# Dense logits in one visit at step 13, four places for the row maxima, lambda's sums two steps earlier

## The reference

```python
qa, ka, va, qi, ki, wi, ga, qb, kb, vb, gb = _split_in(h @ w_in[i])
oa = _dsa_attention(qa, ka, va, qi, ki, wi, top_k)     # sparse: top 64 keys by an indexer
lam_init = 0.8 - 0.6 * math.exp(-0.3 * i)
lam = (jnp.exp(jnp.sum(lambda_q1[i] * lambda_k1[i]))
       - jnp.exp(jnp.sum(lambda_q2[i] * lambda_k2[i])) + lam_init)
ob = _diff_attention(qb, kb, vb, lam, lam_init, subln_g[i])
y = jnp.concatenate([oa * jax.nn.silu(ga), ob * jax.nn.silu(gb)], axis=-1) @ w_out[i]
x = x + _rmsnorm(y, post_norm_g[i])
# then: x = x + rmsnorm((p[i] @ w_ple_proj[i]) * sigmoid(x @ w_ple_gate[i]))

# the dense (differential) group, per block of 128 queries, chunk-causal over 256 keys:
probs = jax.nn.softmax(jnp.where(allowed, logits, NEG_INF), axis=-1)
attn = (probs[:, 0] - lam * probs[:, 1]).astype(v.dtype)
out = _rmsnorm(attn @ v, sub_g) * (1.0 - lam_init)
```

## Time and profile before

| | us |
|---|---|
| median of 3 runs | 357.84 (357.63 to 358.26) |
| the profiled execution | 358.45 |
| its span | 356.7 |
| TensorE's matmuls busy | 348.7 (98% of the span) |
| VectorE busy | 263.6 (74%) |
| ScalarE busy | 229.0 (64%) |
| GpSimd busy | 68.0 (19%) |

### The profile page before, as it was taken

How to read it: one execution, slowest core, us unless ns; L and a number is a source line. 1 busy time by engine, 2 the same in 40 slices (tenths; PEclk the granted TensorE clock), 3 DMA queues, 4 the chain that set the end, 5 groups by cost and what they waited for, 6 DMA issues and landing times.

```text
span 356.7 us, 5705 instructions
## 1 busy us (share of the span) xinstructions
PE 348.7 (98%) x1927; PEld 292.0 (82%) x1927; DVE 263.6 (74%) x562; ACT 229.0 (64%) x459; POOL 68.0 (19%) x121
## 2 busy tenths in 40 slices
PE   8999999999999999999999999999999999999992
PEld 7897888888888788888888888788888888888882
DVE  2886979988875676786797577988895658678543
ACT  4797567686577945555667564787666796365221
POOL 1066351142200000003105624004230000000000
PEclk9999999999999999999999999999999999999997
DMA  7996479862744464657575927546356336550011
GB/s 265 380 360 191 125 224 175 285 173 67 196 160 148 146 195 159 203 167 154 182 226 155 349 82 208 161 122 180 115 146 208 115 130 228 176 169 10 2 48 69
DMA packets 31820, 61.12 MB, mean 171 GB/s; under 512 B 2376, under 2 KB 4432, under 8 KB 31792
## 3 DMA queue, kind: packets, MB, share of 16 engines
q1 hardware_dynamic: 30656, 57.48, 50.3%
q0 software_dynamic: 1120, 3.28, 4.8%
q10 hardware_dynamic: 16, 0.00, 0.0%
HBM read 59.71 MB, written 1.05 MB: 170 GB/s over the span
## 4 chain that ended last, share of the span: by engine, by line
PE 94%; issue 2%; DMA 1%; DVE 1%; ACT 0%; POOLq 0%; DVEq 0%; POOL 0%; SPq 0%
PE proj L1249 26%; PE proj L1251 25%; PE proj L1250 25%; PE sc L1330 3%; PE tr L1398 2%; PE tr L1348 2%; PE sc L1182 2%; PE pv L1415 1%; DMA raw<-in_w_ple_proj_dram 1%; PE proj L1166 1%; PE proj L1193 1%; PE pv L1420 1%; PE proj L1182 1%; PE proj L1262 1%; PE proj L1155 1%
## 5 line engine op out<-in xcount | busy, mean ns | idle before, releaser
L1249 PE MATMUL proj<-w_hi,act_hi 128*128 128x512 f32 (+1 forms) x392 | 157.1, 401 | 0.0
L1251 PE MATMUL proj<-w_hi,act_lo 128*128 128x512 f32 (+1 forms) x392 | 152.2, 388 | 0.0
L1250 PE MATMUL proj<-w_lo,act_hi 128*128 128x512 f32 (+1 forms) x392 | 151.6, 387 | 0.0
L849 DVE TENSOR_TENSOR w_lo<-raw,w_hi 128x1024 fp32r<-128x1024 f32 (+1 forms) x102 | 121.3, 1208 | 10.5 <-ACT w_hi L610 9.9
L610 ACT ACTIVATE w_hi<-raw 128x1024 fp32r<-128x1024 f32 (+2 forms) x103 | 102.4, 1023 | 3.3 <-PE proj L1251 1.8
L1251 PEld LDWEIGHTS proj<-w_hi,act_lo 128*128 128x128 f32 x392 | 73.6, 188 | 15.5
L1249 PEld LDWEIGHTS proj<-w_hi,act_hi 128*128 128x128 f32 x392 | 73.7, 188 | 14.3 <-issue 0.7
L1250 PEld LDWEIGHTS proj<-w_lo,act_hi 128*128 128x128 f32 x392 | 73.8, 188 | 12.8
L551 POOL TENSOR_TENSOR rstd<-var,minus_half 128x1 f32<-128x1 f32 x12 | 7.6, 639 | 190.8 <-DVE var L837 161.4
L746 ACT ACTIVATE probs<-probs,neg_max 128x128 f32<-128x128 f32 (+1 forms) x64 | 28.2, 444 | 4.8 <-DVE neg_max L1000 4.8
L541 POOL TENSOR_TENSOR v_all<-work,rot_tab 128x128 f32<-128x128 f32 x16 | 10.6, 662 | 76.8 <-ACT work L610 76.6
(11 more groups left out here) (229 smaller groups left out, 450.1 us busy)
## 6 DMA issues: line engine op xcount, KB each, us to landing
raw<-in_w_in_dram SPq DMA_DIRECT2D x59, 512.0 KB, 4.1
raw<-in_w_out_dram SPq DMA_DIRECT2D x16, 512.0 KB, 3.3
raw<-in_w_ple_gate_dram SPq DMA_DIRECT2D x16, 512.0 KB, 3.8
raw<-in_w_in_dram SPq DMA_DIRECT2D x7, 324.0 KB, 5.0
raw<-in_w_ple_proj_dram SPq DMA_DIRECT2D x4, 512.0 KB, 4.1
resid<-in_x_dram SPq DMA_DIRECT2D x2, 512.0 KB, 7.1
probs<-in_w_in_dram SPq DMA_DIRECT2D x2, 512.0 KB, 9.3
g_ple<-in_ple_norm_g_dram POOLq DMA_DIRECT2D x2, 512.0 KB, 8.0
```

What stands on the lines that cost most here:

```text
L849: nc.vector.tensor_tensor(w_lo[:, g % SLOTS, 0:nk * cols], landing(g, nk * cols), w_hi[:, g % SLOTS, 0:nk * cols].bitcast(fp32), ALU.subtr ...
L1249: nc.tensor.matmul(ps, src_hi[:, b, k0 + k, :], hi, start=(first_u and k == 0), stop=False)
L1250: nc.tensor.matmul(ps, src_hi[:, b, k0 + k, :], lo, start=False, stop=False)
L1251: last = nc.tensor.matmul(ps, src_lo[:, b, k0 + k, :], hi, start=False, stop=last_k)
```

## The change

- S0 moves from place 12 to 13 and S1 from 15 to 13. TensorE computes the logits of tasks 0 to 5 in one visit behind piece 13. Between the first two tasks and the next two it waits for T KB 1 to be read out.
- Tasks 2 and 3 get the banks `pv` and `tr`. PT0 waits for their maxima.
- `neg_max` has four places; the maxima of task i wait for the exponentials of task i-4.
- lambda's step is split. The product and the sums on VectorE and the exponential on ScalarE move to 13, ahead of S; the wait for all five small loads goes with them. Scaling `g_sub` and `neg_lam` stay at 15 as "neg".
- The first round of topk of block 1 moves from 12 to 14.
- E0 stays at 13, E1 at 16, S2's maxima at 18. `S_WITH` is used nowhere else.

```diff
 PLACE = dict(
-    lam=15,
+    lam=13,
+    neg=15,
-    S=[12, 15, 18, 38, 38, 44],
+    S=[13, 13, 18, 38, 38, 44],
-    topk=[[0, 0, 2, 6, 6, 7, 10, 11], [12, 24, 24, 25, 26, 26, 27, 31]],
+    topk=[[0, 0, 2, 6, 6, 7, 10, 11], [14, 24, 24, 25, 26, 26, 27, 31]],
-S_WITH = {1: [2], 3: [4, 5]}
+S_WITH = {0: [1, 2], 3: [4, 5]}
...
-    rank = {"glu": 0, "PV": 1, "PT": 2, "T": 3, "S": 4, "E": 5, "hv": 6, "hn": 7, "R": 8, "topk": 9,
-            "lam": 10, "t8": 11, "ylo": 12}
+    rank = {"glu": 0, "PV": 1, "PT": 2, "T": 3, "lam": 4, "S": 5, "E": 6, "hv": 7, "hn": 8, "R": 9, "topk": 10,
+            "neg": 11, "t8": 12, "ylo": 13}
...
-        neg_max = sb("neg_max", [P, 2, 4])
+        neg_max = sb("neg_max", [P, 4, 4])
...
-            if i // 2 == 4:
+            if i // 2 in (1, 4):
                 return [pv, tr][i % 2]
             return proj[2 + i % 2] if i // 2 in (2, 5) else sc[i % 2]
...
-            def lambda_of(L):
-
-                lam_init = 0.8 - 0.6 * math.exp(-0.3 * L)
+            def lambda_sums(L):
+
                 dve.wait_ge(small_in, 16 * 5 * (L + 1))
                 link(nc.vector.tensor_tensor(lam_in[:, 0:2, :], lam_in[:, 0:2, :], lam_in[:, 2:4, :], ALU.mult))
                 nc.vector.tensor_reduce(lam_s[:, :], lam_in[:, 0:2, :], AX.X, ALU.add).then_inc(lam_sum, 1)
+
+            def lambda_of(L):
+
+                lam_init = 0.8 - 0.6 * math.exp(-0.3 * L)
                 nc.vector.tensor_scalar(g_sub[:, :], g_sub[:, :], 1.0 - lam_init, None, ALU.mult)
                 dve.wait_ge(lam_exp, L + 1)
...
-                        if L * 12 + i >= 2:
-                            dve.wait_ge(exp_done, L * 12 + i - 1)
+                        if L * 12 + i >= 4:
+                            dve.wait_ge(exp_done, L * 12 + i - 3)
...
                 elif kind == "lam":
+                    lambda_sums(L)
+                elif kind == "neg":
                     lambda_of(L)
...
-                elif kind == "S" and s[1] not in (2, 4, 5):
+                elif kind == "S" and s[1] not in (1, 2, 4, 5):
...
-                    elif s[1] == 1:
+                    else:
                         pe.wait_ge(max_done, L * 12 + 2)
-                    else:
-                        pe.wait_ge(max_done, L * 12 + 4)
                     logits(L, s[1], g, b, keys)
-                    if s[1] == 1:
+                    if s[1] == 0:
+                        pe.wait_ge(tr_out, tr_index(L, ("T", "KB", 1)))
+                        logits(L, 1, 0, 1, SEQ)
                         pe.wait_ge(z_out, L * 8 + 2)
-                        logits(L, 2, g, b, keys)
+                        logits(L, 2, 0, 1, SEQ)
...
                     wait_tr(L, s)
+                    if n == 0:
+                        pe.wait_ge(max_done, L * 12 + 4)
```

More of the change, by code:

```diff
@@ L150, in layer_steps @@
     mid = [[] for _ in range(7 * len(both))]
-    placed = [(PLACE["lam"], ("lam",)), (PLACE["glu"], ("glu", 0))]
+    placed = [(PLACE["lam"], ("lam",)), (PLACE["neg"], ("neg",)), (PLACE["glu"], ("glu", 0))]
     for kind in ("S", "E", "R", "PT", "PV"):
@@ L747, in _ @@
                                                         probs[:, i % 4, j * keys:(j + 1) * keys], ACT.Exp,
-                                                        bias=neg_max[:, i % 2, j:j + 1], scale=-1.0,
+                                                        bias=neg_max[:, i % 4, j:j + 1], scale=-1.0,
                                                         accum_out=row_sum[:, g, b, m:m + 1])
@@ L1002, in _ @@
                                 in1=mask, scale=-1.0, scalar=-TAKEN, op0=ALU.add, op1=ALU.min,
-                                accum_out=neg_max[:, i % 2, j:j + 1])
+                                accum_out=neg_max[:, i % 4, j:j + 1])
                         ins.then_inc(max_done, 1)
```

## The result

The changed kernel takes 361.93 us (median of 6 executions, 360.62 to 364.41), the kernel before 357.84. The ratio is 1.0113, with a 95% interval of 1.0074 to 1.0151: slower by 4.1 us. The profiled execution is the fastest of the six, 360.62 us, and 2.17 over the profiled one of before.

The account below looks back on a forecast made before the run. TensorE, busy 98% of the span, was taken to bound the kernel. Merge saving -0.76, stall +3.11 and clock +1.0 made +3.35 us on the median of 357.84: 361.2 us, range 359.2 to 363.2.

Parts of the forecast that it names:

- The merge saves 0.38 us a layer: TensorE's logits in both layers: one visit of 2.725 us in place of two of 3.105 together, 0.76 us saved in all.
- The merged visit waits for nothing: At step 13, S1's k_lo is there at about 56.8 us, its logits begin near 57.5: 0.7 us to spare.
- The landing 7.8 us behind the issue: Layer 0: g_sub's load, issued at 53.01, lands at 60.8 us; VectorE, asking at 56.8, stands still for 4.0 us.
- The chain of 9.45 us to the mix: VectorE, layer 0, from the landing: mix ends at 70.25, PT0 starts near 70.34; stall 3.1 us, net +2.73.
- ScalarE's copy just in time for PV0: Layer 0: PT0's copy done at 72.1 us, TensorE reaches PV0 at 72.16; zero cost taken, up to 0.5 in the range.
- The clock: TensorE's stall before PT0 in layer 0 can bring the clock to its lower level; price 1.0 us, from 0.9 to 3.5.
- The sum: Whole kernel: -0.76 + 3.11 = +2.35 us with the clock kept, +3.35 with its fall; medians 360.2 and 361.2.
- Forecast: Stall of about 3.1 us at PT0 in layer 0, and the clock falls in or after it: 361.2 us, chance 0.44.
- rival A: The same stall at PT0 in layer 0, but the clock stays up: 360.2 us, chance 0.35.
- Rival B: All five small loads of layer 0 landed by 57.7 us, only the saving is left: 357.1 us, chance 0.07.
- The fixed 2 us and the bytes for a load: g_sub's load in some 2.15 us for 64 KB: landed at 55.2, no stall, sum -0.76; the trace's 7.8 was preferred.

## Why the prediction was right or wrong

Right in direction and mechanism; the size is 0.7 us short: +3.35, or 361.2, was forecast, and +4.1, or 361.93, measured.

- *The merge saves 0.38 us a layer.* Right: -0.36 in layer 1 of the changed kernel, -0.37 in layer 0 with the loads early. As a time it is 0.5 to 0.8 us in three kernels (0.50, 0.63, 0.82), against 0.76; two of the three intervals include no change.
- *The merged visit waits for nothing.* Right: TensorE has only the one new wait.
- *The landing 7.8 us behind the issue.* Right: g_sub's load took 7.8 us again, from 52.68, and VectorE stood 4.06 us (4.0 forecast). That it came out to a tenth is partly luck: in six other traces with the five loads at T KB 0 and nothing ahead of them it is 8.0 to 8.6.
- *The chain of 9.45 us to the mix.* Right: 9.36. The stall was 2.97 against 3.1, and PT0's net shift +2.74 against +2.73.
- *ScalarE's copy just in time for PV0.* Right: done 0.2 us before.
- *The clock.* The mechanism was right, the price of one fall too low. The term was 1.0 us, from the low end of 0.9 to 3.5; the runs show 1.6 (the rows of the kernel with g_sub apart) and 1.8 (the filling of the long stall). The low end counted four matmuls, where the rows show five projections and PV0 at the lower level. Nor do the rows near the start that the price was read from show that level: the granted clock of the kernel before reads 1.00 in every stretch from 0 to 10 us, and only the spacing, 0.45, is like the 0.43 behind a fall. The Trainium skill (TensorE: Matmul & The Clock Gate, Why this matters for your kernels) names an idle gap between bursts as the cause; the runs agree on the cause, with falls at gaps of 2.06, 2.27 and 3.67 us and none in 12 executions with the gap filled, and also show a kernel with a gap of 3.6 us and no fall in four executions.
- *The sum.* With 1.6 in place of 1.0 for the clock it would come to 361.8, near the 361.93, but that closeness is chance: the median is over executions of both kinds. The four with one have a median of 362.4, the two without 360.95, each 0.6 to 0.8 over the sum for its kind (361.8 and 360.2). The kernels that kept the clock say the same: +2.95 with the stall filled and +2.94 with the large loads later, against +2.35. So some 0.6 us is missing from the part without the clock. A landing that is mostly later than 7.8 us makes part of it; the rest is open.
- *Forecast and rival A.* They turned out to be two outcomes of one kernel: four executions with a low clock, two without, one of these the profiled one. Its 360.62 is rival A's sum on the profiled execution, 358.45 + 2.35 = 360.8. The other one without a fall took 361.28, 1.1 over A's 360.2.
- *Rival B (all landed by 57.7)* did not come, but two kernels made it true by moving the loads, and gave 357.43 and 357.17 where it said 357.1.
- *The fixed 2 us and the bytes for a load* (the Trainium skill, DMA: Bandwidth & Descriptors, Anatomy of one DMA) come to 2.15 us, an estimate from that page. The runs show 3.6 us with no small load ahead and 7.8 for the fifth of five; neither agrees, and the first is nearer.

Open: what decides in a single execution whether the clock falls, and what, beside the landing, spreads executions by 2 us without it. Low clocks (under 0.994) came in 4 of 6 executions of the changed kernel, 4 of 4 with p first, 0 of 4 with the large loads later, 4 of 24 in the three kernels whose profiled stall was 1.8 to 2.3 us, 0 of 12 with the stall filled by 13 matmuls, and 0 of 34 in the three kernels without a stall. The kernel before, next to them, had one in 57 (0.992 at 360.57 us), which I cannot explain.

## What to carry to other kernels

A step that is moved up takes its waits with it: look up when each awaited load lands in the trace, and not only that nobody waited for it before. One trace gives one landing: here the same load took 7.8 to 8.6 us, and the stall followed it. A wait for several loads is that for the last of them, and small loads queue behind each other, so issue them where nothing is late, or let the first reader wait only for what it reads. Price a stall of the bounding engine twice, once for its length and once for the clock, and take several executions before trusting the median.

## What the runs showed of the hardware

- A 64 KB load that spreads one row over 128 partitions took 3.6 us to land with no small load ahead of it, and 7.1 to 8.6 in layer 0 behind four of 32 KB each issued in the 2.4 us before (6.2 in layer 1 of the kernel before). Without three large loads behind it, it took 8.5, no less.
- The last of the four lam_in loads seemed to land within 6.0 to 6.8 us where it shared a semaphore with g_sub's, and took 7.4 when counted alone. That parts of the next load completed its count is my reading of it, not shown by one execution.
- The granted clock fell to its lower level in or behind stalls of TensorE of 2.06, 2.27 and 3.67 us, and stayed up through one of 2.97 and one of 3.6. After a fall projections were 0.43 us apart in place of 0.23, and 1.6 to 1.8 us were lost. Useless matmuls in the stall kept it up, in 12 executions of 12, against 8 falls in 10 of the same two kernels without them.
